# Two projections of 640 tokens computed as 512 + 128 columns in place of 320 + 320

## What is computed

```python
def merge(o_dn, o_na, gt, w_pa, w_pb, w_out):
    g_a, g_b = jnp.split(jax.nn.sigmoid(gt), 2, axis=-1)
    return (g_a * (o_dn @ w_pa) + g_b * (o_na @ w_pb)) @ w_out

u = h @ w_in                      # one combined projection
o_dn = deltanet_branch(...)       # branch A, width 1024
o_na = na_latent(...)             # branch B, width 512 (na_context for context tokens)
x = x + gate1 * merge(o_dn, o_na, gt, w_pa, w_pb, w_out)
x = x + gate2 * SwiGLU(RMSNorm(x) * (1 + scale2) + shift2)
```

## Time and profile before

| | |
|---|---|
| median of three runs | 1395.66 us (1395.28 to 1397.66) |
| span of the profiled execution | 1395.5 us |
| TensorE busy with matmuls | 1360.4 us, 97% |
| TensorE busy with weight loads | 1270.9 us, 91% |
| VectorE busy | 811.8 us, 58% |
| ScalarE busy | 672.1 us, 48% |
| GpSimd busy | 218.0 us, 16% |
| DMA queue q1, share of 16 engines' span | 34.7% |
| mean granted TensorE clock | 0.991 of full speed |

### The profile page before, as it was taken

How to read it: one execution, slowest core, us unless ns; L and a number is a source line. 1 busy time by engine, 2 the same in 40 slices (tenths; PEclk the granted TensorE clock), 3 DMA queues, 4 the chain that set the end, 5 groups by cost and what they waited for, 6 DMA issues and landing times.

```text
span 1395.5 us, 26273 instructions
## 1 busy us (share of the span) xinstructions
PE 1360.4 (97%) x10442; PEld 1270.9 (91%) x10442; DVE 811.8 (58%) x1739; ACT 672.1 (48%) x1480; POOL 218.0 (16%) x189
## 2 busy tenths in 40 slices
PE   6999999999999999999999999899999999999998
PEld 4798989989998998999897888899999999999998
DVE  6466655665565566556536566657966434766422
ACT  4463736446373644637356555337655312555321
POOL 1011020202002020200032220000344003444000
PEclk7999999999999999999999999999999999999999
DMA  9643533233333323313326223522232332332332
GB/s 305 204 133 89 154 95 112 56 100 107 90 108 95 104 63 112 96 59 114 119 83 219 69 69 123 165 76 61 61 91 62 104 89 65 92 91 62 84 91 68
DMA packets 202560, 144.49 MB, mean 104 GB/s; under 512 B 8719, under 2 KB 188215, under 8 KB 202183
## 3 DMA queue, kind: packets, MB, share of 16 engines
q1 hardware_dynamic: 202439, 142.82, 34.7%
HBM read 126.77 MB, written 17.99 MB: 104 GB/s over the span
## 4 chain that ended last, share of the span: by engine, by line
PE 91%; ACT 3%; SPq 2%; DMA 2%; issue 1%; DVE 1%; DVEq 0%; ACTq 0%
PE ps L1195 31%; PE ps L1730 17%; PE ps L1767 11%; PE ps L1494 8%; PE ps L1421 2%; PE ps L1717 2%; PE ps L1626 2%; PE ps L1365 1%; PE ps L1428 1%; PE ps L1341 1%; PE ps L1371 1%; PE ps L1594 1%; PE ps L1269 1%; PE ps L1696 1%; PE ps L1440 1%
## 5 line engine op out<-in xcount | busy, mean ns | idle before, releaser
L1195 PE MATMUL ps<-hT_r,WAH_r 128*128 128x320 f32 x912 | 229.0, 332 | 6.4 <-ACT zs L2063 2.4
L1195 PE MATMUL ps<-xT_r,WAH_r 128*128 128x320 f32 x912 | 208.1, 309 | 0.0
L1195 PEld LDWEIGHTS ps<-hT_r,WAH_r 128*128 128x128 f32 x912 | 145.5, 190 | 26.1 <-issue 10.1
L1195 PEld LDWEIGHTS ps<-xT_r,WAH_r 128*128 128x128 f32 x912 | 153.2, 189 | 0.0
L1195 PE MATMUL ps<-hT_r,W_r 128*128 128x320 f32 x592 | 134.2, 310 | 0.0
L1767 PE MATMUL ps<-a_part,W_r 128*128 128x320 f32 x704 | 132.3, 310 | 0.0
L3170 POOL TENSOR_TENSOR gm<-sqkq,dt 128x1280 f32<-128x1280 f32 x8 | 23.5, 2934 | 571.8 <-DVE Xc L2655 499.8
L1767 PEld LDWEIGHTS ps<-a_part,W_r 128*128 128x128 f32 x704 | 110.3, 188 | 0.0
L1730 PE MATMUL ps<-t_big_r,W_r 128*128 128x320 f32 x380 | 107.2, 310 | 0.5 <-ACT naT L2320 0.4
L1730 PE MATMUL ps<-b_part,W_r 128*128 128x320 f32 x456 | 101.3, 309 | 0.0
L1195 PEld LDWEIGHTS ps<-hT_r,W_r 128*128 128x128 f32 x592 | 99.6, 190 | 0.0
(11 more groups left out here) (436 smaller groups left out, 3275.4 us busy)
## 6 DMA issues: line engine op xcount, KB each, us to landing
oT<-in_ffn_w SPq DMA_DIRECT2D x44, 512.0 KB, 5.3
W<-in_w_in SPq DMA_DIRECT2D x36, 512.0 KB, 4.1
WAH<-in_w_ada SPq DMA_DIRECT2D x18, 1024.0 KB, 6.9
naT<-in_w_in SPq DMA_DIRECT2D x24, 512.0 KB, 4.2
oT<-in_ffn_w SPq DMA_DIRECT2D x16, 704.0 KB, 4.7
ext_dram<-naT SPq DMA_DIRECT2D x28, 320.0 KB, 4.1
tA<-ext_dram SPq DMA_DIRECT2D x16, 320.0 KB, 3.6
GCB<-gc_dram SPq DMA_DIRECT2D x7, 640.0 KB, 4.6
```

What stands on the lines that cost most here:

```text
L1195: m = e.matmul(ps[:, bank + b, 0:n], w[:, k, :], x[:, k, a:a + n], start=k == 0 and i == 0, stop=k == KD - 1 and i == 2, skip_group_check= ...
```

## The change

Both projections cut their tokens in 512 + 128 columns, in matmuls and in evictions. The number of matmuls, the banks and all waits stay. Evictions of the second branch projection remain two, of 512 and 128 columns; those of the output projection become two in place of three. The first branch projection, which shares `three`, keeps its halves by the default of the new argument.

```diff
-            def three(bank, big, small, x_big, x_small, k, k_n):
+            def three(bank, big, small, x_big, x_small, k, k_n, tokens=HALVES):
 
                 for i, (w, x) in enumerate(((big, x_big), (big, x_small), (small, x_big))):
-                    for b, (a, n) in enumerate(HALVES):
+                    for b, (a, n) in enumerate(tokens):
                         m = e.matmul(ps[:, bank + b, 0:n], w[:, k, :], x[:, k, a:a + n], start=k == 0 and i == 0, stop=k == k_n - 1 and i == 2, skip_group_check=True)
                 return m
...
                 for i, (w, x) in enumerate(((pb_big[:, n % 2, k, :], na_big[k]), (pb_big[:, n % 2, k, :], naT_r[:, k, :]), (pb_small[n % 4][:, k, :], na_big[k]))):
-                    for b, (a, c) in enumerate(HALVES):
+                    for b, (a, c) in enumerate(SEG):
...
-                    m = three(2 * (n % 3), wo_big[:, n % 4, :, :], wo_small[n % 4], y_big, y_small, k, KD)
+                    m = three(2 * (n % 3), wo_big[:, n % 4, :, :], wo_small[n % 4], y_big, y_small, k, KD, SEG)
...
-                for b, (a, w) in enumerate(HALVES):
+                for b, (a, w) in enumerate(SEG):
                     m = e.scalar_tensor_tensor(yB[:, i, a:a + w], tA[:, i, a:a + w], 1.0, ps[:, 2 * i + b, 0:w], ALU.add, ALU.mult)
...
-                for b, a, w, c in PIECES:
-                    m = e.scalar_tensor_tensor(xT[:, n, a:a + w], ps[:, 2 * (n % 3) + b, a - b * HT:a - b * HT + w], mods[:, 16 + n, c:c + 1], xT[:, n, a:a + w], ALU.mult, ALU.add)
+                for c, (a, w) in enumerate(SEG):
+                    m = e.scalar_tensor_tensor(xT[:, n, a:a + w], ps[:, 2 * (n % 3) + c, 0:w], mods[:, 16 + n, c:c + 1], xT[:, n, a:a + w], ALU.mult, ALU.add)
```

## The result

The changed kernel takes **1405.27 us** (median of four runs, 1403.82 to 1406.26), the kernel before 1395.68 (four runs beside it, 1395.28 to 1397.66). The ratio is 1.0072, interval 1.0059 to 1.0084: 9.6 us slower. The forecast was 1407.2 with a range of 1403.5 to 1412.

A forecast was written before the change was run, and what follows sets the result against it. TensorE was taken to bound the kernel, busy 97% of the span. 240 pairs x 53.1 ns = 12.74, plus 0.5 for the transfer, minus 1.7 for the clock, gave +11.5 us on 1395.66: 1407.2 us, range 1403.5 to 1412.

The forecast's parts named there:

- The load behind a short matmul, 111.7 ns: Both projections: the next long matmul begins one weight load after the 128-column matmul starts, 111.7 ns later, lower end 108.
- I take the excess as a limit on the rate, 0.458 ns a column: 234.6 ns: Both projections: a 512-column matmul takes 234.6 ns, or 226.6 if the 13.3 ns excess is fixed per matmul.
- 48 pairs of blocks n=4 to 7, all on the path (+2.5): Second branch projection, last four blocks: 48 pairs, each 53.1 ns longer, all counted on the path.
- 18 pairs ahead of the transfer (+0.5, between 0 and 0.96): Second branch projection, blocks n=0 and 1: tA transfer issued 0.96 us later, of which 0.5 us taken as arriving.
- 30 pairs hidden: Second branch projection, rest of n=1, n=2 and 3: 1.6 us more, hidden in idle stretches of 0.88 and 3.58 us.
- The clock (-1.7): Blocks n=4 to 7: shorter idle time ahead likelier than not keeps the clock at 2.4 GHz, saving 1.7 us.
- forecast A: Whole kernel: 1407.2 us, from 1404 to 1407.7, with the clock staying at 2.4 GHz; chance 0.50.
- forecast B: Whole kernel: the clock falls all the same, after the restart or elsewhere; +13.2 us, 1408.9; chance 0.32.
- The base: Whole kernel: profiled span of 1395.5 us is within 0.2 us of the median 1395.66, so the sum is set on it.
- Rival D: Both projections: loads run two deep, so 640 columns cost 293.2 ns as now; 1395.7 us; chance 0.03.
- E: Both projections: the 13.3 ns vanishes and loads get by the short matmul, 269.6 ns a pair; 1389.6 us; chance 0.02.
- C: Both projections: a short fp32r matmul is as slow as a plain one, 220 ns; +39 us, about 1433; chance 0.08.

The follow-up runs named there:

- e5: Changed kernel, but in the output projection each block does its 24 long matmuls first, then its 24 short ones; 1406.18 us, ratio 1.0067 to the kernel before.
- e3: Kernel before with both projections cut 448 + 192 columns; 1400.76 us, ratio 1.0030.
- e4: Kernel before with both projections cut 384 + 256 columns; 1395.26 us, ratio 0.9999.
- e6: Changed kernel, but the output projection's 512-column matmuls load only 64 of 128 weight columns (some outputs left out, timing only); 1395.41 us, ratio 1.0001.
- after: First profiled execution of the changed kernel, no further edit; span 1402.9 us, device time 1404.68 us.
- e10: Kernel before, no edit, profiled a third time; one time, 1394.11 us.
- e8: Changed kernel with the xT load cut into eight pieces and issued later; 1404.05 us, ratio 1.0051 to the kernel before.
- e7: Kernel before with the xT load cut into eight pieces and issued later; 1391.99 us, ratio 0.9966.
- e2: Kernel before with only the second branch projection cut 512 + 128; 1396.57 us, ratio 1.0004.
- e11: Changed kernel, no further edit, profiled again; one time, 1405.79 us.
- before: First profiled execution of the kernel before, the one the forecast started from; span 1395.5 us.
- e9: Kernel before, no edit, profiled a second time; one time, 1395.94 us.
- e1: Kernel before with only the output projection and its evictions cut 512 + 128; 1404.83 us, ratio 1.0062.

## Why the prediction was right, and where its sum was off

The direction and the mechanism held, and the time lies in the range: +9.6 us (median) against +11.5. By the steps of the prediction:

- **The load behind a short matmul, 111.7 ns: right.** e5 shows 111 ns from short to short, gave 111 and 113, and 113.3 are left for it in a pair. e3 and e4 put the crossing between 192 and 256 columns, e6 takes the cost away by halving the load. The Trainium skill, page "TensorE: Matmul & The Clock Gate", section "LDWEIGHTS (loading the stationary operand)", gives a load as its weight columns / 1.2 in ns, 107 ns for 128. The loads agree: in the changed kernel those of a pair start 108 ns apart, and 64 columns less make a load 54 ns shorter in e6. The estimate of 271.6 ns a pair, worked out from the formula for a lone stream in its section "Back-to-back issue gap", does not hold here: 340.0 were measured.
- **"I take the excess as a limit on the rate, 0.458 ns a column: 234.6 ns": the step that failed.** The long matmul takes 226.7 ns in a row of its kind (e5), and 340.0 less 111 to 113 is 227 to 229 in a pair of the changed kernel; its load starts split the pair in 108 and 232, where 111 and 235 were forecast. The end that the prediction had named for a fixed cost, 226.6, is the better one, and it fits e3 too. A pair costs 46.8 ns more, not 53.1: 192 x 46.8 = 8.97 us in the output projection instead of 10.2.
- **48 pairs of blocks n=4 to 7, all on the path (+2.5): wrong in what they displace.** The blocks took 15.32 to 15.89 us before and 16.75 after, so +0.9 to +1.4. The matmuls did grow by about the +2.5: from start to start a pair takes 344 ns in this stage of after, 4 more than in the output projection, for which no run shows a reason. But before, part of the time was VectorE's or the half clock's already, and the longer matmuls lie over that. Against the execution that the forecast started from, +2.55 for the pairs and -1.7 for the clock came to +0.85, and 15.89 to 16.75 is +0.86: that agreement is luck, the cancelling of two terms that are both too large.
- **18 pairs ahead of the transfer (+0.5, between 0 and 0.96): nothing.** Issued 0.7 us later, the transfer landed no later behind A. This was the lower end.
- **30 pairs hidden: right, and the 18 with them.** The two idle stretches together went from 0.88 + 2.77 = 3.65 us (e10) to 0.58 + 0.71 = 1.29 (after), 2.36 less, and 48 pairs x 46.8 ns are 2.25. e8 against e7 shows the price without the cover. The idle time ahead of n=4 was forecast at 1.5 to 2.3 us and was 0.71 and 0.90: the forecast started from the 3.58 of one execution with a late landing. From 2.77, 42 pairs (18 and 24) x 46.8 ns = 1.97 leave 0.80.
- **The clock (-1.7): two faults.** The fall was taken from a single execution as a property of the kernel, though the same program kept its clock in e10. And its price was read from the matmuls, without asking what was late next: with VectorE's work right behind it, only 0.56 us of the fall lay on the path. With the new split in this stage no fall came there in six traces (after, e2, e5, e6, e8, e11), with the old split and its idle time it came in two of four (before and e9, not e1 and e10). The two that fell had also fallen near 78 us, the two that did not had not. Of the six with the new split four had that earlier fall (e2, e5, e8, e11) and still kept their clock at n=4. That fits forecast A rather than B; that the shorter idle time prevents the fall is likely from this, not shown.
- **The base.** "The profiled span is within 0.2 us of the median" set a span beside a device time. The device time is 1.8 us above the span in the executions where both are given (1404.68 and 1402.9; 1403.5 and 1401.7), so the profiled execution before stood some 1.6 us above the median, and it contained both clock falls. A -1.7 for a fall that other executions did not have should not have been taken from the median in full.
- **VectorE: right**, 751 against 759 ns, and its saving worth nothing.
- **The range.** Its low end, 1403.5, lies only 0.4 us under the 1403.9 of forecast A, though the text adds some 2 us for the spread of runs; by its own words it would be about 1402. The measured 1405.27 lies in both.

With the terms as measured: 8.97 for the output projection and, against e9 and e10, +0.7 to +1.5 for the stage before it, together 9.7 to 10.4 us, beside the 9.6 of the medians. Single executions alike in their clock say the same: e10 and after, neither with a fall near 78 us, differ by 10.6 us, e9 and e11, both with one, by 9.9. The parts that were over-sized (+1.2, +1.1 to +1.6, +0.5) and the clock (-1.7) partly cancelled, so the total is nearer than its terms. Without the clock term the sum would have been 1408.9, forecast B, which is in the range too, so the total alone could not have told A from B. Rival D (two loads deep) and E (faster) are refuted by 340.0 ns a pair, C by e6. The 1.5 ns a matmul in E's sum stand in no run; where no wide load stood behind the short matmul, a pair still took 286.8 ns (e6), not 269.6.

## What to carry to other kernels

When every matmul brings its own weight load, cut the moving columns so that the shortest part still runs for as long as one load takes: with 128 weight columns that was reached at 256 columns (384 + 256 is free), and 448 + 192 cost 5 us, 512 + 128 9.6 us, over some 240 pairs. Before a term is written for a clock fall or a late transfer, look at what is late next and at more than one execution. A transfer that a chain waits for should not stand in the queue behind a bulk load that is needed later: cutting that load and issuing it later (e7) gave 3.7 us, more than any split did.

## What the runs showed of the hardware that was not expected

- **The time over columns / 2.4 does not grow with the width.** Sustained spacing of fp32r matmuls with 128 weight columns, where no load holds them: 384 + 256 columns in 293.3 ns a pair (26.6 over for the two), 320 in 146.6 (13.3 over), 512 in 226.7 in e5 (13.3 over). The pair of 512 and 128 columns in e6 has 286.8 - 266.7 = 20.1 over for both, so the short one less. From 320 to 512 columns this is a fixed 13.3 ns a matmul, which the prediction had ruled out because the half clock shows nothing on top; both stand, and nothing here shows the cause. In the changed kernel the two matmuls of a pair are recorded 60 and 280 ns apart, although its loads stand 108 and 232 apart and e5 has 111 for a short one: a recorded start can come before the weights are there, so only sums over a pair, or rows of like beside like, were used.
- **The clock falls or stays in the same program after the same 2.77 us of idle time** (e9 and e10), and the other fall near 78 us comes in about half of the executions of either kernel. Between e10 and e9 the stage A to B moved by 0.55 us and the start A by 1.2 (857.49 and 858.71; the opening of the kernel may have its share in that, which was not taken apart).
